# A recurrent mixer trunk with every engine's program written out for all eight blocks, and the bank adds moved ahead of the last weight split

## The reference, cut to what matters

```
h = rms_norm(x, norm_w) * (1.0 + scale) + shift
p = h @ w_in                       # gq gk gv gz lr hq hf hi hz mg
o_g = chunk_gated_state(gq, gk, gv, log_a);  o_h = chunk_gated_state(silu(hq), k_h, hi, log_f)
m = g_a * (o_g @ w_up_gla) + g_b * (o_h @ w_up_hgrn)
x = x + gate * (m @ w_out)
return rms_norm(x, final_norm_w)
```

## Time and profile before

| | |
|---|---|
| median of 3 runs | 2849.99 us (2847.86 to 2850.46) |
| profiled execution, own time | 2851.12 us |
| its span | 2849.3 us |
| TensorE busy | 2801.4 us, 98% of the span |
| VectorE, ScalarE, GpSimd busy | 58%, 48%, 11% |
| mean granted TensorE clock | 0.995 |

### The profile page before, as it was taken

One profiled execution on the slowest core, in us unless ns is written; L12 is line 12 of the kernel. 1 busy time (PEld: TensorE's weight loads), 2 busy tenths in 40 slices (PEclk: granted clock), 3 DMA queues, 4 the chain that ended last, 5 costly groups with the idle time before them and its releaser, 6 DMA issues.

```text
span 2849.3 us, 38285 instructions
## 1 busy us (share of the span) xinstructions
PE 2801.4 (98%) x14328; PEld 2297.1 (81%) x14328; DVE 1653.7 (58%) x2122; ACT 1353.5 (48%) x1763; POOL 301.1 (11%) x415
## 2 busy tenths in 40 slices
PE   6999999999999999999999999999999999999998
PEld 4888888788887888878888888888888888888886
DVE  7765475644656456564565636646376463755636
ACT  4643357434573345633456434564345643465334
POOL 1531100101001010010100110001100011000101
PEclk9999999999999999999999999999999999999999
DMA  8532363233622345323452235422354223532224
GB/s 338 207 128 97 126 216 95 76 104 130 212 89 82 104 152 190 96 75 119 166 164 93 75 126 173 155 90 75 125 182 147 90 75 126 196 131 90 79 99 148
DMA packets 100678, 373.15 MB, mean 131 GB/s; under 512 B 11440, under 2 KB 11696, under 8 KB 98928
## 3 DMA queue, kind: packets, MB, share of 16 engines
q1 hardware_dynamic: 97040, 358.62, 37.6%
q0 software_dynamic: 3168, 11.54, 1.1%
q10 hardware_dynamic: 256, 0.20, 0.0%
HBM read 345.99 MB, written 24.12 MB: 130 GB/s over the span
## 4 chain that ended last, share of the span: by engine, by line
PE 95%; DVE 2%; issue 2%; ACT 1%; DMA 1%; SPq 0%; POOL 0%; POOLq 0%; ACTq 0%; DVEq 0%
PE F L1232 32%; PE A L1221 31%; PE A L1283 12%; PE A L1305 9%; PE F L1221 2%; PE F L1305 2%; PE R L1335 1%; PE F L1362 1%; PE A L1377 1%; PE F L1356 1%; DMA ada_w<-in_ada 1%; PE R L1328 1%; DVE h_tmp L831 0%; DVE w_lo L824 0%; DVE xy L1022 0%
## 5 line engine op out<-in xcount | busy, mean ns | idle before, releaser
L824 DVE TENSOR_TENSOR w_lo<-w_raw,w_hi 128x1024 fp32r<-128x1024 f32 x528 | 658.2, 1248 | 912.2 <-ACT w_hi L578 911.1
L578 ACT ACTIVATE w_hi<-w_raw 128x1024 fp32r<-128x1024 f32 x528 | 557.3, 1057 | 652.8 <-PE A L1221 347.8
L1232 PE MATMUL F<-h_hi,w_hi 128*128 128x512 f32 x1408 | 553.8, 393 | 0.0
L1232 PE MATMUL F<-h_lo,w_hi 128*128 128x512 f32 x1408 | 548.2, 389 | 0.0
L1232 PE MATMUL F<-h_hi,w_lo 128*128 128x512 f32 x1408 | 548.2, 389 | 0.0
L1221 PE MATMUL A<-w_hi,h_hi 128*128 128x512 f32 (+1 forms) x1408 | 532.8, 378 | 2.1 <-issue 2.1
L1221 PE MATMUL A<-w_lo,h_hi 128*128 128x512 f32 (+1 forms) x1408 | 523.1, 371 | 0.0
L1221 PE MATMUL A<-w_hi,h_lo 128*128 128x512 f32 (+1 forms) x1408 | 522.8, 371 | 0.0
L1232 PEld LDWEIGHTS F<-h_hi,w_hi 128*128 128x128 f32 x1408 | 264.3, 188 | 56.2 <-ACT gates L692 1.4
L1221 PEld LDWEIGHTS A<-w_hi,h_hi 128*128 128x128 f32 x1408 | 264.4, 188 | 55.6 <-issue 8.7
L1232 PEld LDWEIGHTS F<-h_lo,w_hi 128*128 128x128 f32 x1408 | 264.4, 188 | 55.4 <-issue 1.7
(11 more groups left out here) (215 smaller groups left out, 3507.6 us busy)
## 6 DMA issues: line engine op xcount, KB each, us to landing
w_raw<-in_w_stream SPq DMA_DIRECT2D x400, 512.0 KB, 3.5
w_raw<-pieces SPq DMA_DIRECT2D x112, 512.0 KB, 3.9
xy<-in_x SPq DMA_DIRECT2D x32, 512.0 KB, 6.1
result<-xy SPq DMA_DIRECT2D x32, 512.0 KB, 2.7
xf<-in_xt SPq DMA_DIRECT2D x30, 512.0 KB, 4.7
xn<-in_x SPq DMA_DIRECT2D x28, 512.0 KB, 4.9
ada_w<-in_ada SPq DMA_DIRECT2D x12, 1024.0 KB, 17.3
w_raw<-in_w_stream SPq DMA_DIRECT2D x16, 544.0 KB, 5.2
```

Source lines behind the costliest of these rows:

```text
L578: AF(w_hi[:, s % RING, 0:n], w_raw[:, r, 0:n], ACT.Copy).then_inc(w_hi_done.sem, 1)
L824: V.tensor_tensor(w_lo[:, s % RING, 0:n], w_raw[:, RAW_AT[s], 0:n], w_hi[:, s % RING, 0:n].bitcast(fp32), ALU.subtract).then_inc(w_split.s ...
L1232: last = mm(dst[:, :], w_[iw][:, s % RING, k * P:(k + 1) * P], h_[ia][:, k, :], start=(k == 0 and n == 0), stop=(k == KT - 1 and n == 2))
```

## The change

All five engines' programs are written out for the eight blocks, with no loop and no jump left. The semaphore counts that the loops computed in registers become constants. Nothing else in the blocks' instructions changes, but for one thing: in slot 65 VectorE does the four bank adds right after it has seen the slot done, before `split_lo`, instead of after it.

```
-            body(0, False, first=True)
-            with sp.Fori(1, NB - 1) as b:
-                body(b, False)
-            body(NB - 1, True)
+            for b in range(NB):
+                body(b, b == NB - 1, first=(b == 0))
...
-            with act.Fori(0, NB - 1) as b:
-                body(b, False)
-            body(NB - 1, True)
+            for b in range(NB):
+                body(b, b == NB - 1)
...
+            def bank_adds(b, i):
+
+                if i in (3, 6):
+                    dve.wait_ge(xy_in[i // 6].sem, xy_in[i // 6].at(b, 32))
+                for pair_, tt, t, half, behind in ADDS[i]:
+
+                    if behind:
+                        dve.wait_ge(y_add.sem, y_add.at(b, behind))
+                    tile = xy(t)[:, half * 512:half * 512 + 512]
+                    V.tensor_tensor(tile, tile, OUT_BANK[pair_][tt][:, :], ALU.add).then_inc(y_add.sem, 1)
...
+                    if s == SLOTS - 1:
+                        bank_adds(b, s - OUT0)
                     if not (last and s + RING >= SLOTS):
                         split_lo(b if s + RING < SLOTS else b + 1, (s + RING) % SLOTS)
...
-                    if s - OUT0 in ADDS:
-                        i = s - OUT0
...
+                    if s - OUT0 in ADDS and s < SLOTS - 1:
+                        bank_adds(b, s - OUT0)
```

More of the change, by code:

```diff
@@ L553, in body @@
                     inverse_root(y_rs[:, t:t + 1], y_ss[:, t:t + 1], y_rstd)
-            body(0, False, first=True)
-            with pool.Fori(1, NB - 1) as b:
-                body(b, False)
-            body(NB - 1, True)
+            for b in range(NB):
+                body(b, b == NB - 1, first=(b == 0))
         @block.scalar
```

## The result

The changed kernel takes 2831.96 us (median of 6, 2831.35 to 2832.81), the kernel before 2848.97 us (median of 6, 2846.23 to 2850.46). That is 17.0 us less in the medians. The ratio is 0.9941 with a 95% interval of 0.9928 to 0.9954 (ratios rest on all runs and can differ by some 0.0003 from that of the medians). The profiled span went from 2849.3 to 2829.8 us, 19.5 less. The runs also lie closer together: 1.5 us apart where those of before are 4.2 apart.

A forecast was written before the change was run, and what follows sets the result against it. TensorE, busy 98% of the span, was taken as the bound, losing time at six jumps back. Span 2849.3 - 18.9 = 2830.4 us; with execution overhead and median, forecast 2831.5 us, range 2828.5 to 2838.

The forecast's parts named there:

- The bound and its reading: At block boundaries: the six with jumps back cost 18.90 us more than the seventh; all of it would be won.
- sample boundary: Block 6 to 7, where engines leave their loops without jumping back; period 346.81 us, taken as what every boundary becomes.
- TensorE's jump: At block heads: the taken branch lasts 5.0 us in the median; block 2 shows waits of 1.59 and 1.19 us.
- ScalarE's pause: After a block's last square: 2.80 us idle plus 1.28 us table load; TensorE waits 2.41 us at block 1's slot 3.
- the two are alternatives: At blocks 2, 4 and 5 TensorE's own stall hides ScalarE's; they are not a sum and both must go.
- The clock: Behind the gaps at 411 and 1794 us: half speed for 3.4 and 3.5 us, 3.4 us lost in all.
- The moved adds: Slot 65: h 1.8 us earlier, split 0.5 us later; priced at 0, bounds 12.6 us gained to 3.5 lost.
- The written-out code: In the block bodies: constant counts and program fetch priced at 0, with TensorE's program reads unchanged.
- A: Rival at slot 3: part of ScalarE's pause stays, 0.7 us at seven boundaries; 2836 to 2840 us, chance 0.07.
- B: Rival at block heads: stalls come from reading new program, not the jump, and stay; 2848 to 2852 us, chance 0.05.
- C: Rival in block bodies: straight code outruns its fetch, 1.6 us per uncovered packet crossing; sixteen give 2857 us; chance 0.05.
- the last step of my sum: From the profiled execution's 2832.2 us, or 2831.1 by the runs' median, to a forecast of 2831.5 us.

The follow-up runs named there:

- Experiment 2: All five programs written out as in the changed kernel, but the adds left behind the split; 2831.87 us.
- experiment 1: Kernel before with all loops kept, only the four bank adds of slot 65 moved ahead of the weight split; 2842.28 us, ratio 0.9981.
- experiment 4: Kernel before with only ScalarE's program written out, adds last; 2843.18 us, ratio 0.9983.
- experiment 9: Changed kernel with TensorE's loop put back, the other four programs written out, adds first; 2845.3 us.
- experiment 3: Kernel before with only TensorE's program written out, the other four looped, adds last; 2853.07 us, ratio 1.0016.
- experiment 10: Changed kernel plus 36 extra TensorE matmuls, results unread, while it waits for the first h; 2829.93 us.
- experiments 6 to 8: Extra ScalarE copies per block: two with all written out and adds last, 2836.30 us; two, then four, in the changed kernel, 2831.54 and 2838.02 us.
- experiment 5: Kernel before with TensorE's and ScalarE's programs written out, SyncE, GpSimd and VectorE looped, adds last; 2834.18 us.

## Why the prediction was right, point by point

**The bound and its reading.** That six boundaries cost 18.90 us over the seventh was the whole forecast. The span fell by 19.5. The changed kernel's periods are all that of the sample boundary, 0.15 us shorter still. The forecast, 2831.5 us, lies 0.5 from the median. It was read, not modelled: the loop's exit was a ready sample of a boundary without a jump. Experiment 2 shows that the whole gain is that of the loops.

**TensorE's jump.** Shown by experiments 1, 4 and 9: one or two waits at each jump as long as TensorE has its loop, whatever the others do (eight, ten and eight waits at five jumps), and none once it has not. That it is a fetch of program is borne out by the queue that carries it: three packets in some 10 us at the jump, the first two landing 1.9 and 1.4 us before the two matmuls that had waited, where straight code reads one in some 25 us; and the branch lasts 5 us only when taken.

**ScalarE's pause, and that the two are alternatives.** Shown by experiment 3, slower than before by 0.16%, and by 4. At the pause the queue of the other programs carries three packets where it carries one without ScalarE's loop, so the pause reads as a fetch too. The pause (2.80 us) and the table load (1.28) were not separated on the chip. Against a slack of 1.5 us, the load alone, 1.28, would be hidden with the adds last, by the measured slack; that is argued only.

**The clock.** The low stretches behind the gaps went with the gaps; experiment 3 brought four of them in place of two, and experiment 10 removed the one at the head with work that computes nothing. Between the head and the end each stands behind a wait of 2.1 to 2.4 us, but another wait of 2.1 us has none behind it (experiment 3).

**The moved adds.** Priced at nothing with 1.8 us of earlier h: experiment 2 gives 0 for the time, experiments 6 to 8 give 1.9 us for the slack. Where the cover is gone, because ScalarE is late by the loops, the moved adds alone gain 6 us (experiment 1), inside my bound of 12.6.

**The written-out code.** Two small things were off. The packets of TensorE's program fell from 128 to 114; I had them unchanged. They are 114 whenever TensorE's own program is written out (experiment 3 too) and 128 whenever it is looped (experiment 4). About two of the 14 are instructions that are gone (29666 on TensorE before, 29167 after, 256 to a packet of 16 KB). The other twelve are two to three at each of five jumps, which reads as code fetched and then not run. And the written-out code was not quite free of effect inside the blocks: the wait of the small matmul at L1170, 1.7 us over seven, is 1.2 at L1168, and the period fell from 346.81 to 346.66. In experiments 4 and 5, where VectorE's, GpSimd's and SyncE's programs are looped, the last period is still 346.77. So up to 0.15 us a block, 1 us in all, belongs to these programs; which of them, no run tells. It accounts for the 0.6 us by which the span fell further than 18.9: 1.05 us over seven periods, less 0.33 by which the first run of slots 17 to 19 began later (143.86 against 143.53), and less 0.1 behind the last.

**The rivals.** A (something of ScalarE's pause stays) did not come, nor did B or C: 2774 us at full clock have no wait in the list but 1.2 us. The runs also explain the last step of my sum, the choice between the profiled execution and the median. The runs of before vary by their stalls, and those of the changed kernel hardly vary, so the median gained 17.0 us where the profiled execution gained 19.5; the stall-free time lies near 2832 whichever one starts from.

## What to carry to other kernels

A loop around a long body is not free on a queue that must never run dry: look for the one boundary where the loop is left and compare its period with the others, and you have the loop's price before any edit (18.9 us here, and the span fell by 19.5). Write out all engines on the path, not the busiest alone: taking one of two stalls at the same place away can leave the other, in one longer piece, and be slower (experiment 3). An order that is worth nothing in time may still be worth slack; a dose of dummy work, with a second order beside it, measures that in two runs.

## What the runs showed of the hardware that was not expected

A taken jump costs a different amount each time: with TensorE alone looped, ten runs lie over 8.9 us, with nothing looped six runs lie over 1.5. Where the other engines have loops too, the spread is smaller: 4.9 us over eleven runs in experiment 1 and 4.4 in experiment 4; why is not shown. Experiment 4, with four loops and the adds last, came out at 2843.18, 2 us faster than experiment 9 with one loop (1.4 us if each is held against the kernel before in its own job). The runs overlap, and whether the other engines' loops have a part in it stays open.

The row of the branch does not show the cost on every engine. TensorE's lasts 4.0 to 5.8 us when taken. ScalarE's lasts 0.05 us at every jump of the kernel before, and its pause of 2.5 to 2.8 us stands as idle time before the next instruction.

A wait of TensorE that is the jump's can be put down to an engine that happened to finish something just before: it stands as "issue" in the earlier trace rows and as VectorE's `xy` in experiments 1 and 9. The place (a block's head) tells it, and so does the code, which does not ask for that add.
